# A retention and latent-attention encoder step: gates, branches and output product as seven block products for eight

## What is computed

```python
xn = rms_norm(x, norm_mix_w)
rq, rk, rv, rg, cq, ckv, kpe, ga, gb = split_columns(xn @ w_in)
...
ret_y, mla_y, new_state = mixer_core(rq, rk, rv, q, ckv, kpe, w_ukv)
ret_branch = (head_group_norm(ret_y, ret_gn_w) * jax.nn.silu(rg)) @ w_ret_o
mla_branch = mla_y @ w_mla_o
merged = jax.nn.sigmoid(ga) * ret_branch + jax.nn.sigmoid(gb) * mla_branch
h = x + merged @ w_out
g, u = jnp.split(rms_norm(h, norm_ffn_w) @ w_gate_up, 2, axis=-1)
h = h + (jax.nn.silu(g) * u) @ w_down
```

## Time and profile before

| | us |
|---|---|
| three timed runs | 2106.09, 2110.5, 2110.77 (median 2110.5) |
| the profiled execution | 2109.2 |
| its span, first to last instruction | 2107.4 |
| PE busy | 2035.1 |
| DVE busy | 1077.6 |
| ACT busy | 664.7 |
| POOL busy | 330.8 |

### The profile page before, as it was taken

One profiled execution on the slowest core, in us unless ns is written; L12 is line 12 of the kernel. 1 busy time (PEld: TensorE's weight loads), 2 busy tenths in 40 slices (PEclk: granted clock), 3 DMA queues, 4 the chain that ended last, 5 costly groups with the idle time before them and its releaser, 6 DMA issues. The chain is left out here.

```text
span 2107.4 us, 33465 instructions
## 1 busy us (share of the span) xinstructions
PE 2035.1 (97%) x13418; PEld 1963.6 (93%) x13418; DVE 1077.6 (51%) x1900; ACT 664.7 (32%) x1201; POOL 330.8 (16%) x303
## 2 busy tenths in 40 slices
PE   8989999999999999999999999989999999999997
PEld 8978788878999889999999999889999999999997
DVE  6567776765545535422223245665555555432257
ACT  5334444442222233312111124443434343310010
POOL 0110000001212210000000001254444444200000
PEclk9999999999999999999999999999999999999999
DMA  8301111143121212211151114322323232673412
GB/s 306 120 27 42 37 42 37 42 162 117 54 67 47 65 49 89 84 40 46 47 207 50 40 43 154 103 93 93 117 91 117 90 121 87 239 255 118 173 53 85
DMA packets 89134, 202.77 MB, mean 96 GB/s; under 512 B 11696, under 2 KB 42352, under 8 KB 86192
## 3 DMA queue, kind: packets, MB, share of 16 engines
q1 hardware_dynamic: 89008, 201.01, 27.9%
HBM read 142.27 MB, written 58.70 MB: 95 GB/s over the span
## 5 line engine op out<-in xcount | busy, mean ns | idle before, releaser
L866 PE MATMUL ps<-xn_hi,w_hi 128*128 128x384 f32 (+1 forms) x960 | 318.4, 332 | 5.6 <-DMA xn_lo<-xn_spill 2.9
L866 PE MATMUL ps<-sx_hi,t_hi 128*128 128x272 f32 x1056 | 306.4, 290 | 12.1 <-ACT u L1597 5.9
L868 PE MATMUL ps<-xn_lo,w_hi 128*128 128x384 f32 (+1 forms) x960 | 315.4, 329 | 0.0
L867 PE MATMUL ps<-xn_hi,w_lo 128*128 128x384 f32 (+1 forms) x960 | 315.0, 328 | 0.0
L867 PE MATMUL ps<-sx_hi,t_lo 128*128 128x272 f32 x1056 | 306.1, 290 | 0.0
L868 PE MATMUL ps<-sx_lo,t_hi 128*128 128x272 f32 x1056 | 304.9, 289 | 0.0
L866 PEld LDWEIGHTS ps<-sx_hi,t_hi 128*128 128x128 f32 x1056 | 200.8, 190 | 13.1 <-issue 6.9
L867 PEld LDWEIGHTS ps<-sx_hi,t_lo 128*128 128x128 f32 x1056 | 200.7, 190 | 0.1
L868 PEld LDWEIGHTS ps<-sx_lo,t_hi 128*128 128x128 f32 x1056 | 200.6, 190 | 0.0
L866 PEld LDWEIGHTS ps<-xn_hi,w_hi 128*128 128x128 f32 x960 | 181.6, 189 | 10.8 <-DMA xn_lo<-xn_spill 5.4
L867 PEld LDWEIGHTS ps<-xn_hi,w_lo 128*128 128x128 f32 x960 | 182.0, 190 | 0.0
(11 more groups left out here) (263 smaller groups left out, 4712.3 us busy)
## 6 DMA issues: line engine op xcount, KB each, us to landing
w_stage<-in_weights SPq DMA_DIRECT2D x83, 512.0 KB, 3.8
y_spill<-hg_r SPq DMA_DIRECT2D x44, 544.0 KB, 3.4
yd<-y_spill SPq DMA_DIRECT2D x22, 1088.0 KB, 5.8
raw<-in_weights SPq DMA_DIRECT2D x22, 512.0 KB, 5.2
hg<-in_weights SPq DMA_DIRECT2D x22, 512.0 KB, 5.3
d_stage<-in_weights SPq DMA_DIRECT2D x24, 384.0 KB, 3.2
ym_spill<-out_hl SPq DMA_DIRECT2D x32, 256.0 KB, 2.4
xt<-in_x SPq DMA_DIRECT2D x8, 544.0 KB, 8.3
```

The source lines that it names most:

```text
L866: nc.tensor.matmul(out, wh, xh, start=start, stop=False, skip_group_check=onto)
L867: nc.tensor.matmul(out, wl, xh, start=False, stop=False, skip_group_check=onto)
L868: return nc.tensor.matmul(out, wh, xl, start=False, stop=stop, skip_group_check=onto)
```

## The change

The six products of 1024 x 1024 become six "octets" (`OCTETS`). Each is cut in 2 x 2 x 2 blocks: output features in two halves of 4 tiles, input features in two halves of 4 tiles, tokens in two halves of 544. Seven block products (`STEPS`) take the place of eight. A step has 4 units (one per pair of output tiles `p` and `p + 4`), a unit is 24 matmuls of 272 columns, so an octet has 28 units (`UNITS`).

- *Activations.* The four blocks and four sums of them (S1 to S4) are put in DRAM, one array of 7 operands for each source: `s_x` for the three gates, `s_yg` and `s_ym` for the branches, `s_m` for the output product. SP streams one operand per step into a ring of three (`operand_load`), and ACT and DVE split it there in two parts (`operand_octet`).
- *Where the sums are made.* Those of `x` and of the heads' results `ym` during retention, in eight turns of four chunks: SP loads two whole tiles (`prep_load`), ACT multiplies them by the norm gain in the first four turns (`prep_gains`), POOL sums (`prep_sums`), SP stores 7 tiles (`prep_store`). Those of `yg` (the gated retention) during the octet `GATE_A`. Those of the merged activations on POOL at the end of `BRANCH_MLA` and the start of `MIX_OUT` (`merged_sums`).
- *Weights.* Each unit has its own 4 blocks, a row of 512 columns, split by ACT and DVE three units ahead in a ring of four (`weights_octet`); 16 sums per octet on POOL (`octet_sums`), of which 8 stand at the end of the octet before.
- *Results.* Four quadrants per octet. Three are first copied to `hg` by ACT and completed by DVE with the last steps' results, then scaled, gated or added; what other octets need goes through DRAM (`yg_spill`, `gate_spill`), and the other factor comes in pieces of 544 columns.
- *Attention.* The heads' results are stored whole (`out_f`, one ACT copy) and no longer as a high and a low part; the loads of the normed activations for retention are issued earlier in SP's order.
- *Opening of the feed-forward part.* The sums of its activations are all made on POOL (`up_sums`), and the first pair runs its products in the order 0, 3, 2, 1, 4, 5, 6. The squares for its norm are summed on POOL too.

```diff
-                        n = o_index(h, pair)
-                        w = DEC if pair == 4 else 2 * P
-                        u = p_order["M", h, "O", pair]
-                        dve.wait_ge(p_high, high_index["M", h, "O", pair] + 1)
-                        low(out_hl[n % 2][:, 1, 0:w], ps[:, unit_bank(u), 0:w],
-                            out_hl[n % 2][:, 0, 0:w]).then_inc(p_free, 1)
...
+            def prep_store(q):
...
+                if q < 4:
+                    sp.wait_ge(prep_gain, 2 * q + 2)
+                sp.wait_ge(prep_done, 4 * q + 4)
+                for i, src in enumerate((tiles[0][:, lower], sums[1], sums[2], tiles[1][:, upper], tiles[1][:, lower],
+                                         sums[0], sums[3])):
+                    sp.dma_start(target[i, :, q % 4, :], src).then_inc(prep_out, 16)
...
+                    if s[0] == "B":
+                        turn, at_turn = divmod(9 * h + s[1], 4)
+                        if at_turn == 0 and turn:
+                            prep_store(turn - 1)
+                        if at_turn == 0 and turn < 8:
+                            prep_load(turn)
+                        if s[1] == 7 and h == RH - 1:
+                            first_loads()
...
+            def octet_unit(o, s, p):
...
+                pe.wait_ge(ot_low, n + 1)
...
+                elif s < 4:
+                    pe.wait_ge(o_copy, 12 * o + 4 * (s - 1) + p + 1)
+                else:
+                    pe.wait_ge(o_read, 16 * o + 4 * (s - 4) + p + 1)
+                th, tl = t_hi[n % 4], t_lo[n % 4]
+                for half in range(2):
+                    cols = slice(QUARTER * half, QUARTER * (half + 1))
+                    for k in range(4):
+                        if p == 0 and half == 0 and k % 2 == 0:
+                            pe.wait_ge(so_low, 2 * j + k // 2 + 1)
+                        last = product(ps[:, 2 * p + half, 0:QUARTER], th[:, k, :], tl[:, k, :],
+                                       s_hi[j % 3][:, k, cols], s_lo[j % 3][:, k, cols], k == 0 and opens, k == 3, not opens)
+                last.then_inc(oct_done, 1)
...
                     elif s[0] == "B":
+                        if n == 0:
+                            for b in range(2):
+                                act.wait_ge(o_out[b], 16 * 20)
+                        if n % 4 == 1 and n < 16:
+                            prep_gains(n // 4)
+                        if n == 9 * RH - 2:
+                            for u in range(3):
+                                weights_octet(u)
+                        if n == 9 * RH - 1:
+                            for part_of in range(2):
+                                operand_octet(0, part_of)
                         act.wait_ge(z_done, n + 1)
...
+                    late, m = divmod(g - 3, UNITS)
...
+                    if late == BRANCH_MLA and 16 <= m < 20:
+                        merged_sums("S3", m - 16)
+                    if late == BRANCH_MLA and m >= 24:
+                        merged_sums("S4", m - 24)
+                    late, m = divmod(g - 2, UNITS)
+                    if late == BRANCH_MLA and 20 <= m < 24:
+                        merged_sums("S1", m - 20)
+                        merged_sums("S2", m - 20)
+                    if late == BRANCH_MLA and 12 <= m < 20:
+                        branches_added(m - 12)
```

More of the change, by code:

```diff
@@ L476, in build, with all_free @@
         ATT_END = p_order["M", MH - 1, "O", 3] + 1
+        own, outs = [0], [0]
+        for key in p_order:
+            out = key[0] == "M" and key[2] == "O"
+            own.append(own[-1] + (not out))
+            outs.append(outs[-1] + out)
+        def all_free(engine, u):
+            engine.wait_ge(p_free, own[u])
+            if outs[u]:
+                engine.wait_ge(o_free, outs[u])
         rotated = [k for k in p_order if (k[0] == "M" and k[2] == "R") or (k[0] == "R" and k[2] in "QK")]
@@ L482, in build @@
         high_index = {k: i for i, k in enumerate(
-            [k for k in p_order if k[0] == "M" and k[2] != "R"])}
+            [k for k in p_order if k[0] == "M" and k[2] not in "RO"])}
         def unit_bank(u):
@@ new lines, in first_loads @@
+            def first_loads():
+                sp.wait_ge(w_low, I_OCT)
+                sp.wait_ge(z_done, 9 * (RH - 1))
+                for half in range(2):
+                    row_load(0, 0, half)
+                sp.wait_ge(prep_out, 16 * STEPS * 8)
+                operand_load(0)
+                sp.wait_ge(p_done, p_order["R", RH - 1, "V", 8] + 1)
+                for r in (3, 1):
+                    for half in range(2):
+                        row_load(0, r, half)
+                operand_load(1)
+                for half in range(2):
+                    row_load(0, 2, half)
@@ L785, in _ @@
-            sp.wait_ge(s_low, S2B_AT)
-            sp.wait_ge(s_sum_p, S4_SUM_AT[3])
+            for octet in range(OCTETS):
+                for n in range(UNITS):
+                    octet_transfers(octet, n)
+            octet_transfers(OCTETS, 0)
+            octet_transfers(OCTETS, 1)
+            octet_transfers(OCTETS, 2)
+            sp.wait_ge(s_low, S2_AT)
+            sp.wait_ge(s_sum_p, S4_SUM_AT)
             pair_load(1)
@@ L833, in _ @@
             sp.wait_ge(q_done, last + 7)
+            for t in range(6, KT):
+                residual_load(t)
             for half in range(2):
@@ L1176, in _ @@
+            for o in range(OCTETS):
+                for s in range(STEPS):
+                    for p in range(4):
+                        octet_unit(o, s, p)
             stationary = ((t01_hi, t01_lo, 0), (t01_hi, t01_lo, 1), (t2_hi, t2_lo, None), (t35_hi, t35_lo, 0),
@@ L1179, in seven_products @@
             def seven_products(pair):
-                for j, name in enumerate("XYXZXZX"):
+                for j in FIRST_ORDER if pair == 0 else range(7):
+                    name = "XYXZXZX"[j]
                     pe.wait_ge(tw_low, 5 * pair + (1, 1, 2, 3, 4, 3, 5)[j])
@@ L1207, in seven_products @@
                     last.then_inc(q_done, 1)
-                    if pair == 0 and j in (2, 6):
-                        pe.wait_ge(summed, SUM_OUT + 24)
-                        for g in (0, 1) if j == 2 else (2,):
+                    if pair == 0 and j in (1, 4):
+                        pe.wait_ge(sq_sum, 14)
+                        pe.wait_ge(o_read, 16 * OCTETS)
+                        for g in (0, 1) if j == 1 else (2,):
                             c0, c1 = GROUPS[g]
@@ L2400, in _ @@
+            all_free(pool, ATT_END)
             for h in range(RH):
@@ L2454, in _ @@
+            for i in (13, 14, 15):
+                squares_added(i)
+            for p in range(4):
+                up_sums("S4", p)
             for pair in range(UP_PAIRS):
```

1133 lines of the change are left out of this document (702 added, 431 removed).

## The result

The changed kernel takes 2124.49 us (median of 4 runs, 2122.99 to 2126.87) where the kernel before takes 2108.82 on the same chip: a ratio of 1.0074, 95% interval 1.0061 to 1.0087. It is slower by 0.7%; 2080 us was forecast, and 2042 to 2112 as the range.

What follows compares the result with a forecast made beforehand. The rewritten stage was taken as bound by TensorE's instructions. From 2109.2 us, -70.6 + 3.4 - 9 + 11 + 3 + 6 + 3 + 15 + 9 = -29.2 gave 2080 us, range 2042 to 2112.

Steps and rivals of the forecast that it cites:

- Products (-70.6): Gates, branches and output product: 4032 matmuls at 0.12504 us take 504.2 us against 574.8, -70.6 us.
- Attention (-9): Attention: heads' results no longer split, 6 us, and retention's activations fetched earlier, 3 us; -9 together, from 0 to -18.
- Retention's scalings (+11 and +3): Retention turns 1 and 3: ScalarE's scalings await a load ahead of the chunk's copy, +11 us; half clock after, +3.
- End of retention (+6): Last two chunks: weight and operand splits ahead of the chunk's copies delay the next stage, +6 us (0 to 10).
- Stage's joints (+3 and +15): VectorE and GpSimd exclude each other at SBUF: +3 us after the first octet, +15 from MLA branch to output product.
- Feed-forward opening (+9): First pair's second product waits for GpSimd's S1 and S2, and the same chain follows: +9 us (0 to 16).
- rival 2: Octets' ends: VectorE, blocked by GpSimd, falls behind at each of five joints, +57 us, 2137 us; chance 0.09.
- Rival 3: Octets: each of 42 steps waits 1 us for its operand and loses as much to the clock, 2164; chance 0.04.

Runs made afterwards that it cites:

- split_back: Changed kernel plus one VectorE instruction per heads' result, with the structure of the split taken out: 2131.95 us, 1.0109 of the kernel before.
- gain_after: Changed kernel with ScalarE's two scalings of the x tiles behind the chunk's copies: 2124.96 us, 1.0082 of the kernel before.
- spread: Changed kernel, scalings behind copies, five quarters of sums in retention in turns of 6 chunks, seven in GATE_A and GATE_B: 2103.07 us, 0.9969 of the kernel before.
- spread_end: 'spread' with first turn's stores behind the weight items, first octet's splits behind the last copies, late quarters some units earlier: 2100.86 us, 0.9965 of the kernel before.
- narrow_pool: Changed kernel, GpSimd's weight sums, gatings, branch, merged and late sums cut to 8 columns from the second octet on: 2092.09 us, 0.9926 of the kernel before.
- narrow_joint: Changed kernel, only GpSimd's 24 branch and merged sums at the MLA branch's end cut to 8 columns: 2109.08 us, 1.0000 of the kernel before.
- squares_dve: Changed kernel, opening's S2 on VectorE before weight splits, GpSimd's squares' sums after S1's split, last seven on VectorE: 2118.08 us, 1.0042 of the kernel before.

## Why the prediction was wrong, step by step

The measured time lies 12.5 us above the range. The products were priced right; the waits that the change adds in retention, in the stage and in the opening were not.

- **Products (-70.6): right.** 4032 matmuls, octets of 84.2 us where nothing waits (84.0 by the sum).
- **Attention (-9): right way, mis-sized, -13.1.** The split's 6 are 6.7 by the start of the projections (473.6 to 466.9), 7.5 by 'split_back'. The other 6.4, for the 3 of the loads, lie between there and retention (78.0 to 71.6 us): the wait of 1.60 us went, and with it the stretch at half clock behind it. No run puts the loads back in their old place; that the gain is theirs is read from these rows alone. They show 18 us around the start of the projections, before and after, with the granted clock in the last column but two:

```profile
473.00:491.00 18.00, 15.39 (x56) 11.70 (x57) 5.31 (x10) 2.80 (x5) 1.02 (x1) 0.72 0.70 265
```

```profile
466.00:484.00 18.00, 16.62 (x104) 15.55 (x103) 10.87 (x21) 3.94 (x8) 3.07 (x2) 1.00 0.24 78
```

- **Retention's scalings (+11 and +3): the step that failed in kind.** The prediction saw that SP "waits until these have landed" and followed only the tile behind that wait. It had to name all that stands behind it in SP's list: the chunk's weight items. Two readings were also too low by themselves. Chunk 5's copy moves from 587.13 to 594.8, which is 7.7 us and not 7. And turn 3 sets the end of a copy (645.4) against the start of a chunk (641.14); with the 2.3 us that lie between chunk 5's copy and chunk 6 it is 6.5 and not 4.5. Turn 1 cost 13.2 us with its clock for 7 predicted, turn 3 7.0 for 4.5, and turn 4, counted as free since it has no scalings, 10.1 (3.5 us came back later, where the kernel before was idle and this one was not). 'gain_after' shows that the scalings' place on ScalarE is worth nothing in total. 'spread' gains 21 us, with three quarters less in retention, and 'spread_end' removes the last stalls there by order alone.
- **End of retention (+6): right**, 8.1. TensorE waited 5.55 and 4.54 us there, behind the splits.
- **Stage's joints (+3 and +15): right mechanism, mis-sized.** The last joint took 21.8 us for 15, the first octet's end 6.8 for 3. The step that failed there is "VectorE then lags some 3 us where 5.5 are to spare": the gatings, 1.74 us each on GpSimd in the first octet's span, meet VectorE's 2.7 of 3.0 us in every unit from the sixteenth on, so the lag is not made in the last four units only: the chain that ended last runs on VectorE from 849.7 us on, 33 us before the octet ends. The end of GATE_A (9.2 us) was not in the sum at all: GpSimd's late quarters hold SP, and the operands' loads stand behind them, as in retention. 'narrow_pool' gives back 32 of the stage's 41 us, by shorter turns and a shorter chain together, 'narrow_joint' 16.6 of the joint's 21.8. The Trainium skill, "SBUF — State Buffer", section "Who interferes with whom", has the lock as exclusive; the runs agree, with 1578 against 715 ns in the mean for the same 544 columns.
- **Feed-forward opening (+9): the wait was right, what follows was not.** TensorE went on at +19.9 for +21. The step that failed is "from there both follow the same chain". It holds only for what hangs on that product. The sums of squares and S4, and with them the roots and the second pair's loads, hang on GpSimd; the table load for the roots came 17 us later, and the whole was +22. Of the 22 us, 'squares_dve' gives back 7 and some 15 stay open.
- **Rivals.** The time falls where rival 2 (each octet's end pays, 2137) was to decide, above 2117, but not by its mechanism alone: two of five ends paid by it and one through SP, and 15 us of the excess are retention's. Rival 3, the stream late at each step, is out: 'narrow_pool' moves the same bytes, and its first five octets take 423.5 us for the 421.0 that they would without a wait.

The 44 us between 2080 and 2124 are thus 15 in retention, 20 in the stage and 13 in the opening, less 4 in attention: that attention gained more than was counted is luck for the number.

## What to carry to other kernels

When an edit adds a wait to a queue, list what stands behind it in program order until the next free slot, and price each by who needs it; here what waited for the edit's own data was not the worst. A place where an engine waits for that queue already, in the trace of before, is where to look first. Where VectorE and GpSimd share a way into SBUF, add their instructions over each few units as if on one engine, in every place where the two sums come near the time there, and not only in the worst. And when a chain is late, ask of every later join which of its inputs hang on the late engine, for one repaired wait gives way to the next.

## What the runs showed of the hardware

- In 'spread_end' ScalarE's copy stood 10.72 us for the landing of two small stores (128 x 128 fp32 each), asked for behind 4.2 MB of loads (six of 512 KB, one of 1088). Here what was asked for ahead of a transfer said more on when it landed than its size.
- VectorE's 12 products of 544 columns with both inputs in SBUF took either 0.71 to 0.72 us or 1.82 to 1.88 us beside GpSimd's sums, and nothing between; in 'narrow_pool', with GpSimd at 8 columns, all 12 took 0.71 to 0.73.
- All 16 DMA engines can be busy (share 1.01) at 355 GB/s, and a load of 1088 KB then lands after 8.8 us (asked for at 949.93, split at 958.71) for the 5.8 of the earlier trace rows. The 322 GB/s of the earlier trace rows, by which the prediction times its stores, were no ceiling: 'narrow_pool' moved 391 GB/s for 15 us. That the transfers' rate was taken too low did not make the loss.
